# Seven block products in place of eight in the down projection of the second feed-forward

## The reference, cut to what matters

```
y = jnp.square(jax.nn.relu(h @ ffn_w1[i])) @ ffn_w2[i]
x = x + g2 * rmsnorm(y, norm_g[i, 3])
```

## Time and profile before

| | us |
|---|---|
| median of 3 runs | 2071.27 (2071.01 to 2071.88) |
| span of the profiled execution | 2068.0 |
| PE busy | 2035.2 (98%) |
| DVE busy | 1153.0 (56%) |
| ACT busy | 859.5 (42%) |
| POOL busy | 110.2 (5%) |
| chain that ended last: on PE | 94% |
| `ffn1`, from its first up tile to its last down tile | about 345 |

### The profile page before, as it was taken

One profiled execution on the slowest core, in us unless ns is written; L12 is line 12 of the kernel. 1 busy time (PEld: TensorE's weight loads), 2 busy tenths in 40 slices (PEclk: granted clock), 3 DMA queues, 4 the chain that ended last, 5 costly groups with the idle time before them and its releaser, 6 DMA issues.

```text
span 2068.0 us, 27825 instructions
## 1 busy us (share of the span) xinstructions
PE 2035.2 (98%) x10894; PEld 1699.1 (82%) x10894; DVE 1153.0 (56%) x1758; ACT 859.5 (42%) x1291; POOL 110.2 (5%) x100
## 2 busy tenths in 40 slices
PE   7999999999999999999999999999999999999998
PEld 5898888888887888988888888876777798888887
DVE  4667867566565345654233335436679746546455
ACT  3334472424246222356233246345455545324233
POOL 0000000000001025110000001000111000000000
PEclk9999999999999999999999999999999999999999
DMA  9572337576553423423332331511132132323321
GB/s 315 163 242 85 127 111 238 192 226 198 171 167 115 152 77 102 113 82 102 102 101 83 101 112 56 150 52 31 45 117 84 43 112 96 109 81 102 102 72 71
DMA packets 230377, 248.32 MB, mean 120 GB/s; under 512 B 10978, under 2 KB 223357, under 8 KB 229365
## 3 DMA queue, kind: packets, MB, share of 16 engines
q1 hardware_dynamic: 187968, 202.45, 30.8%
q10 hardware_dynamic: 42293, 44.27, 6.6%
HBM read 237.63 MB, written 8.42 MB: 119 GB/s over the span
## 4 chain that ended last, share of the span: by engine, by line
PE 94%; DVE 2%; ACT 1%; DMA 1%; issue 1%; DVEq 1%; SPq 0%; ACTq 0%; POOL 0%; POOLq 0%
PE bank L615 37%; PE bank L687 32%; PE bank L789 4%; PE bank L1254 4%; PE bank L718 2%; PE bank L859 2%; PE bank L1226 1%; PE bank L1003 1%; PE bank L1237 1%; PE bank L1201 1%; PE bank L1310 1%; PE bank L1295 1%; PE bank L1204 1%; PE bank L1124 1%; PE bank L754 1%; DMA ada_head<-in_ada_w 1%
## 5 line engine op out<-in xcount | busy, mean ns | idle before, releaser
L615 PE MATMUL bank<-h_hi,w_both_hi 128*128 128x512 f32 x528 | 206.6, 391 | 0.0
L615 PE MATMUL bank<-h_hi,w_both_lo 128*128 128x512 f32 x528 | 205.5, 389 | 0.0
L615 PE MATMUL bank<-h_lo,w_both_hi 128*128 128x512 f32 x528 | 205.5, 389 | 0.0
L1380 ACT ACTIVATE u_both_hi<-raw 128x2048 fp32r<-128x2048 f32 x62 | 117.1, 1906 | 174.3 <-PE bank L687 134.4
L1988 DVE TENSOR_TENSOR u_both_lo<-raw,u_both_hi 128x2048 fp32r<-128x2048 f32 x62 | 141.6, 2290 | 84.9 <-ACT u_both_hi L1380 84.9
L1988 DVE TENSOR_TENSOR w_both_lo<-raw,w_both_hi 128x2048 fp32r<-128x2048 f32 x62 | 142.0, 2290 | 74.6 <-ACT w_both_hi L1380 74.5
L615 PE MATMUL bank<-h_hi,u_both_hi 128*128 128x512 f32 x464 | 180.9, 390 | 0.0
L615 PE MATMUL bank<-h_lo,u_both_hi 128*128 128x512 f32 x464 | 180.6, 389 | 0.0
L615 PE MATMUL bank<-h_hi,u_both_lo 128*128 128x512 f32 x464 | 180.6, 389 | 0.0
L1380 ACT ACTIVATE w_both_hi<-raw 128x2048 fp32r<-128x2048 f32 x62 | 117.4, 1907 | 143.5 <-PE bank L687 91.8
L687 PE MATMUL bank<-u_both_hi,g_hi 128*128 128x512 f32 x408 | 160.1, 392 | 0.0
(11 more groups left out here) (455 smaller groups left out, 4495.9 us busy)
## 6 DMA issues: line engine op xcount, KB each, us to landing
raw<-in_ffn_w SPq DMA_DIRECT2D x64, 1024.0 KB, 5.2
ada_raw<-in_ada_w ACTq DMA_DIRECT2D x40, 1024.0 KB, 5.2
raw<-in_w_up SPq DMA_DIRECT2D x22, 1024.0 KB, 5.1
raw<-in_b_w_in SPq DMA_DIRECT2D x16, 1024.0 KB, 5.4
raw<-in_w_in SPq DMA_DIRECT2D x15, 1024.0 KB, 5.5
raw<-in_a_w_in SPq DMA_DIRECT2D x12, 1024.0 KB, 6.4
ada_head<-in_ada_w SPq DMA_DIRECT2D x8, 1024.0 KB, 12.3
raw<-in_b_w_out SPq DMA_DIRECT2D x8, 1024.0 KB, 6.3
```

Source lines behind the costliest of these rows:

```text
L615: mm = pe.matmul(o, x, y, start=(k == 0 and j == 0), stop=(k == kc - 1 and j == 2))
L1380: act.activation(slot(where, s)[0], raw[s][:], ACT.Copy).then_inc(sem("hi_done"), 1)
```

## The change

In groups 0, 1 and 2 of `ffn1` (`FAST = 3`) the down half is worked as one step of a Strassen-Winograd scheme. The hidden values of a group are a matrix A of 512 tokens x 1024, cut in quarters (`quarter(tok, k)`), the weights a matrix B of 1024 x 1024, cut in quarters B11, B12, B21, B22 of 512 x 512 (one 1 MB tile each). In place of eight products of quarters there are seven, m0 to m6, of quarters or sums of quarters. A product is 2 token blocks x 4 k-steps x 3 passes = 24 matmuls with 512 moving columns, so the down half has 168 matmuls in place of 192. The fourth group stays as it was.

Items of a group in PE's order, each with a split weight tile: u0, u1, u2, u3 (the up tiles, items 0 to 3), then m0 to m6 (items 4 to 10). Item by item the B side is B11, T1, T2, B22, T3, B21, T4, where the sums are made in place in the raw buffers by POOL with 128x2048 additions: T1 = B11 + B12, T2 = T1 + B22, T3 = B12 + B22, T4 = T2 + B21. POOL also makes `lo` of items 7 (B22) and 9 (B21), and one A-side difference S3 (128x1024). On the A side the hidden values are kept in full (`g32`: Relu and Square, no rounding); for each product ACT rounds a quarter or a sum into one of three `a_slot`s (128x1024) and DVE makes its `lo`; DVE makes the sums S1 (in two halves of 128x512), S2 and the next one (128x1024 each) in `s_sum`. Four raw buffers stand in place of two, and a ring of three split slots (W0, W1, U0) in place of four, because U1 is the room of raw buffers 2 and 3.

Products use banks 0 and 1 (even m) or 2 and 3 (odd m) and partly go on adding to what the bank holds. DVE adds the bank of each token block to `Y` after each product: 14 additions in a group in place of 8, and PE starts product m only when those of product m-2 are done. On PE, DVE, ACT and POOL the three groups are written out, without the loop. The rest of the change only merges semaphores.

```diff
-PHASES = [("a_in", 12, 2), ("a_out", 4, 2), ("ffn0", 32, 2), ("b_in", 16, 2), ("b_out", 8, 2), ("ffn1", 32, 2),
+PHASES = [("a_in", 12, 2), ("a_out", 4, 2), ("ffn0", 32, 2), ("b_in", 16, 2), ("b_out", 8, 2), ("ffn1", 10, 2),
...
+FAST = 3
+FAST_RING = [("W", 0), ("W", 1), ("U", 0)]
+FAST_NAMES = ["u0", "u1", "u2", "u3", "B11", "B12", "B22", "B21"]
+FAST_RAW = [[0, 1, 0, 1, 2, 3, 0, 1], [0, 3, 1, 2, 0, 3, 1, 2], [1, 3, 2, 0, 1, 3, 2, 0]]
+FAST_FROM = ["B11", "B11", "B11", "B22", "B12", "B21", "B11"]
+FAST_POOL = ["T1", "S3", "T2", "T3", "lo B22", "T4", "lo B21"]
...
+def fast_low(g, i):
+    if i in (7, 9):
+        return "f_pool", 7 * g + FAST_POOL.index("lo B22" if i == 7 else "lo B21") + 1
+    return "f_lo", sum(1 for n in range(2, 11 * g + i + 1) if n % 11 not in (7, 9))
...
+        f_raw = raw + [at("raw2", "U", [P, TILE], F32, 8192), at("raw3", "U", [P, TILE], F32, 24576)]
+        g32 = at("g_full", "G", [P, KB, S])
+        a_slot = [[at(f"a_{part}{i}", reg, [P, 4, HALF], F32R, off + 4096 * j) for j, part in enumerate(("hi", "lo"))]
+                  for i, (reg, off) in enumerate((("G", 16384), ("G", 24576), ("AD", 0)))]
+        s_sum = at("s_sum", "S2", [P, 4, HALF])
+        s3_sum = at("s3_sum", "C", [P, 4, HALF])
...
+        def fast_slot(n):
+            return slot(*FAST_RING[n % 3])
+        def quarter(tok, k):
+            return g32[:, 4 * k:4 * k + 4, tok * HALF:tok * HALF + HALF]
...
+            def fast_split(g, i):
+                which, n = fast_low(g, i)
+                sp.wait_ge(sem(which), n)
+            for g in range(FAST):
+                if g == 0:
+                    sp.wait_ge(sem("split_done"), t0 + 1)
+                else:
+                    fast_split(g - 1, 7)
+                    sp.wait_ge(sem("f_pool"), fast_pool(g - 1, "T3"))
+                    fast_in(g, "u0", cols(w1, g * 1024, 256))
+                    fast_split(g - 1, 8)
+                    fast_in(g, "u1", cols(w1, g * 1024 + 256, 256))
+                    fast_split(g - 1, 9)
+                    sp.wait_ge(sem("f_pool"), fast_pool(g - 1, "T4"))
+                fast_in(g, "u2", cols(w1, g * 1024 + 512, 256))
+                if g == 0:
+                    sp.wait_ge(sem("split_done"), t0 + 2)
+                else:
+                    fast_split(g - 1, 10)
+                fast_in(g, "u3", cols(w1, g * 1024 + 768, 256))
+                rows = cols(w2[:, g, :], 0, D)
+                if g == 0:
+                    sp.wait_ge(sem("block_done"), N0["ffn1"])
+                else:
+                    fast_split(g, 0)
+                fast_in(g, "B11", rows[:, 0:4, 0:512])
+                if g:
+                    fast_split(g, 1)
+                fast_in(g, "B12", rows[:, 0:4, 512:1024])
+                fast_split(g, 2)
+                fast_in(g, "B22", rows[:, 4:8, 512:1024])
+                fast_split(g, 3)
+                fast_in(g, "B21", rows[:, 4:8, 0:512])
...
+            def fast_up(g, j):
+                which, n = fast_low(g, j)
+                pe.wait_ge(sem(which), n)
+                wh, wl = (w.rearrange("p (k n) -> p k n", k=KB) for w in fast_slot(11 * g + j))
+                for b in range(2):
+                    m, bs = 2 * (j % 2) + b, slice(b * P, b * P + P)
+                    if j < 2:
+                        pe.wait_ge(sem("f_added"), 14 * g - (1 - b if j == 0 else 3 - b))
+                    else:
+                        pe.wait_ge(sem("f_g"), 8 * g + m + 1)
...
+            def fast_product(g, m):
+                which, n = fast_low(g, 4 + m)
+                pe.wait_ge(sem(which), n)
+                pe.wait_ge(sem("f_a_lo"), 8 * g + [1, 3, 4, 5, 6, 7, 8][m])
+                wh, wl = (w.rearrange("p (k n) -> p k n", k=4) for w in fast_slot(11 * g + 4 + m))
+                ah, al = a_slot[(7 * g + m) % 3]
+                for c in range(2):
+                    if m < 2:
+                        pe.wait_ge(sem("f_g"), 8 * g + 4 + 2 * m + c + 1)
+                    else:
+                        pe.wait_ge(sem("f_added"), 14 * g + 2 * (m - 2) + c + 1)
+                    cs = slice(c * P, c * P + P)
+                    for k in range(4):
+                        for i, (x, y) in enumerate([(ah, wh), (ah, wl), (al, wh)]):
+                            mm = pe.matmul(bank[2 * (m % 2) + c][:], x[:, k, cs], y[:, k], start=(k == i == 0 and m in (0, 1, 5)),
+                                           stop=(k == 3 and i == 2), skip_group_check=True)
+                    mm.then_inc(sem("f_product"), 1)
...
+            for g in range(FAST):
+                for j in range(0 if g else 2, 4):
+                    fast_up(g, j)
+                for m in range(7):
+                    fast_product(g, m)
...
+            def fast_free(n):
+                g, i = divmod(n - 3, 11)
+                if n == 2:
+                    act.wait_ge(sem("block_done"), 4 * q0)
+                elif n < 5:
+                    act.wait_ge(sem("block_done"), 4 * q0 + 2 * i + 2)
+                elif i < 4:
+                    act.wait_ge(sem("f_up"), fast_block(g, 2 * i + 1))
+                else:
+                    act.wait_ge(sem("f_product"), 14 * g + 2 * (i - 4) + 2)
...
+            for g in range(FAST):
+                fast_hi(g, 2)
+                fast_hidden(g, 0)
+                fast_hidden(g, 1)
+                fast_hi(g, 3)
+                fast_hidden(g, 2)
+                fast_hidden(g, 3)
+                fast_hi(g, 4)
+                act.drain()
+                fast_a(g, 0, quarter(0, 0))
+                fast_hidden(g, 4)
+                fast_hidden(g, 5)
+                fast_hi(g, 5)
+                act.wait_ge(sem("f_s"), 4 * g + 1)
+                fast_a(g, 1, s_sum, slice(0, 2))
+                fast_hidden(g, 6)
+                fast_hidden(g, 7)
+                act.wait_ge(sem("f_s"), 4 * g + 2)
+                fast_a(g, 1, s_sum, slice(2, 4))
+                fast_hi(g, 6)
+                act.wait_ge(sem("f_s"), 4 * g + 3)
+                fast_a(g, 2, s_sum)
+                fast_hi(g, 7)
+                act.wait_ge(sem("f_s"), 4 * g + 4)
+                fast_a(g, 3, s_sum)
+                fast_hi(g, 8)
+                act.wait_ge(sem("f_pool"), fast_pool(g, "S3"))
+                fast_a(g, 4, s3_sum)
+                fast_hi(g, 9)
+                fast_a(g, 5, quarter(0, 1))
+                fast_hi(g, 10)
+                fast_a(g, 6, quarter(1, 1))
+                for i in range(2):
+                    if g < FAST - 1:
+                        fast_hi(g + 1, i)
...
+            def fast_s1(g, ks):
+                dve.wait_ge(sem("f_g"), 8 * g + 4 + ks.stop)
+                dve.tensor_tensor(s_sum[:, ks], quarter(1, 0)[:, ks], quarter(1, 1)[:, ks], ALU.subtract).then_inc(sem("f_s"), 1)
...
+            def fast_add(g, m, c, row, part, op):
+                dve.wait_ge(sem("f_product"), 14 * g + 2 * m + c + 1)
+                o, b = Y[:, row + c, part * 512:part * 512 + 512], bank[2 * (m % 2) + c]
+                if g == 0 and m in (0, 1, 6):
+                    dve.tensor_copy(o, b[:]).then_inc(sem("f_added"), 1)
+                elif g == 0 and m == 2:
+                    dve.tensor_scalar(o, b[:], -1.0, None, ALU.mult).then_inc(sem("f_added"), 1)
+                else:
+                    dve.tensor_tensor(o, o, b[:], op).then_inc(sem("f_added"), 1)
...
+            for g in range(FAST):
+                for i in (2, 3, 4):
+                    fast_lo(g, i)
+                fast_a_lo(g, 0, 1, quarter(0, 0))
+                fast_lo(g, 5)
+                fast_s1(g, slice(0, 2))
+                fast_a_lo(g, 1, 2, s_sum, slice(0, 2))
+                fast_s1(g, slice(2, 4))
+                fast_a_lo(g, 1, 3, s_sum, slice(2, 4))
+                dve.drain()
+                dve.tensor_tensor(s_sum[:], s_sum[:], quarter(0, 0), ALU.subtract).then_inc(sem("f_s"), 1)
+                fast_lo(g, 6)
+                fast_a_lo(g, 2, 4, s_sum)
+                for c in range(2):
+                    fast_add(g, 0, c, 0, 0, ALU.add)
+                dve.tensor_tensor(s_sum[:], s_sum[:], quarter(0, 1), ALU.add).then_inc(sem("f_s"), 1)
+                for c in range(2):
+                    fast_add(g, 1, c, 2, 1, ALU.add)
+                fast_a_lo(g, 3, 5, s_sum)
+                fast_lo(g, 8)
+                fast_a_lo(g, 4, 6, s3_sum)
+                for c in range(2):
+                    fast_add(g, 2, c, 0, 1, ALU.subtract)
+                fast_a_lo(g, 5, 7, quarter(0, 1))
+                dve.drain()
+                for c in range(2):
+                    fast_add(g, 3, c, 0, 1, ALU.add)
+                fast_lo(g, 10)
+                fast_a_lo(g, 6, 8, quarter(1, 1))
+                for c in range(2):
+                    fast_add(g, 4, c, 2, 1, ALU.subtract)
+                if g < FAST - 1:
+                    fast_lo(g + 1, 0)
+                else:
+                    rest(u0, 0, "W")
+                for c in range(2):
```

(74 more changed lines are left out.)

106 lines of the change are left out of this document (89 added, 17 removed).

## The result

The changed kernel takes 2085.76 us (median of 4 runs, 2082.66 to 2086.99), the kernel before 2071.14 (4 runs): a ratio of 1.0072, 95% interval 1.0058 to 1.0085, so 0.7% slower. The forecast was 2085.0, 2075 to 2095.

What follows compares the result with a forecast made beforehand. The prediction took ffn1 as bound by PE's number of matmuls, 0.2267 us each. From 2068.0, -16.3 for matmuls and +30 for stalls gave 2081.7; with 3.3 from span to median, 2085.0 us, range 2075 to 2095.

Steps and rivals of the forecast that it cites:

- The rate and the matmuls: Three down halves of ffn1: 72 matmuls fewer at an unchanged 0.2267 us each, 16.3 us saved.
- What was costed at nothing: Groups 0 to 2: leaving the loop, added DVE and ACT work, split slots and loads, all covered by PE's matmuls.
- The exclusion: POOL and DVE instructions with two SBUF inputs hold each other off whole; +30 us in three groups, chance 0.74.
- two short cases: Profile before: DVE's 2.28 us lo stretched POOL's 1.28 to 3.39; POOL's instruction stretched DVE's 0.68 to 1.18.
- the stepping: One down half worked through instruction by instruction: stalls 1.8, 5.3 and 3.2 us, 10.3 a group, 31 in three.
- the releaser it named: The gaps before m1 and m3 were to end with DVE's lo of a_slot; no separate size.
- The third gap: Before m4: additions of m2 stand behind a lo held by POOL's lo of B21; 3.2 us a group.
- the first two gaps: Before m1 and m3: DVE's sums and lo wait for POOL's long instructions; 1.8 and 5.3 us a group.
- The sum: Whole kernel: -16.3 + 30 = +13.7 us, giving 2081.7 for the span and 2085.0 for the median.
- No exclusion for long instructions: Rival: POOL's long instructions don't hold DVE off, nothing is late, 16.3 us won in full, 2055; chance 0.13.
- In part: Rival: DVE is let in within a long POOL instruction; 2 to 5 us a group, 2061 to 2070; chance 0.06.
- Something more: Rival: also POOL's fp32r lo or in-place addition takes 5.0 us or more; +22, 2093 and above; chance 0.07.

Runs made afterwards that it cites:

- the first experiment: Changed kernel with POOL's six 128x2048 instructions of each group cut to 16 columns, all waits kept: 2056.13 us, ratio 0.9928 to the kernel before.
- the run with memsets: Changed kernel with POOL's six 128x2048 instructions of a group replaced by memsets of the same tiles: 2056.53 us, ratio 0.9936 to the kernel before.
- the last experiment: Changed kernel with DVE's two additions of m2 to Y moved ahead of the lo of product 4: 2082.40 us, ratio 1.0062 to the kernel before.
- with quarters: Changed kernel with each of POOL's 128x2048 instructions cut into four of 128x512: 2083.63 us, ratio 1.0064 to the kernel before.
- With halves: Changed kernel with each of POOL's 128x2048 instructions cut into two of 128x1024: 2072.85 us, ratio 1.0012 to the kernel before.

## Why the prediction was right

**The rate and the matmuls.** -16.3 us for 72 matmuls at 0.2267 us: the runs without exclusion show 38.08 us for 168, and `ffn1` from the end of its first pair to its last down tile takes 266.59 us in the first experiment (945.74 to 1212.33) against 282.90 before, 16.3 less.

**What was costed at nothing** (leaving the loop, 14 us more work for DVE and 9 for ACT in a group, three slots, the loads) is nothing: the same run has all of it and no gap.

**The exclusion.** The reading of two short cases carried over to 4.6 us instructions. The gaps before m1 and m3 stand in all three groups, where the stepping put them; the profile puts them down to `issue`, but m1 and m3 start 0.1 us behind the end of DVE's `lo` of `a_slot` (1065.82 and 1081.53 in the second group), the releaser it named. The third gap is there in the first two groups, released by an addition to `Y`, and all but gone in the last (0.1). The table counts groups from 0, so group 1 is the second.

| group 1 | stepped | measured |
|---|---|---|
| before m1 | 1.8 | 1.4 |
| before m3 | 5.3 | 4.7 |
| before m4 | 3.2 | 0.7 |
| m3 at a lower clock | 0 | 2.2 |
| group longer than 81.6 | 10.3 | 9.3 |
| three groups | 31, taken as 30 | 28.0 |

The rows of the second group add up to 9.0; the first matmuls behind a gap follow each other more slowly (0.31 us from the one of 1089.99 to the next in place of 0.2267), which is part of the other 0.3.

(28.0: from 946.49 to 1197.49 are 251.0 us, and 984 matmuls at 0.2267 are 223.0.) The rule of the Trainium skill, SBUF — State Buffer, section Summary: rules for kernel authors, that the one that issues second is blocked until the first has finished, agrees with the trace: DVE's third sum of 1071.59, 1.22 us long by itself, waited until POOL's 4.82 us were over. The same page, section Who interferes with whom, says that a DVE instruction with two SBUF inputs contends with a GpSimd instruction that reads SBUF and not with one that only writes; the run with memsets agrees (1.22 us beside 1.81).

**What was mis-sized.** POOL holds DVE for 4.4 us from the moment DVE lets it in, not 4.5 to 4.6, and ACT's 128x1024 copy takes 1.06 in place of 1.14; worked through the same steps these make up about the 1.0 us by which the first two gaps are shorter. The third gap was forecast at 3.2 and is 0.7: after 4.7 us without work PE ran m3 slower, and so it came to m4 later by itself. As m4 waits for a fixed chain on DVE, the slower matmuls were free. The three groups bear this out: m3 takes 1.6, 2.2 and 2.8 us more than its 5.44, the gap before m4 is 1.3, 0.7 and 0.1, and the sum is 2.9 each time. The prediction had no term for the clock; that it cost nothing here is luck.

**The sum.** The stage is 11.6 us longer where 13.7 were forecast (946.49 to 1241.01 is 294.52, before 282.90). The profiled execution is 12.9 longer as a whole, the medians 14.6. The close hit of the median, 2085.8 against 2085.0, is therefore partly luck: stalls forecast 2 us too long, and some 3 us that the sum didn't have. Of these, 1.3 lie outside the stage in the two profiled executions (12.9 against 11.6), nearly all behind it. The rest is in the other three executions, whose spans are 2083.7 to 2085.2 and whose mean granted clock is 0.991 to 0.993, against 0.994 in the profiled one and 0.997 before. That more of PE's work ran at the lower clock there is likely; no profile of them shows where. The experiments show one such place, though the kernel is the same there in all: in seven of the eight profiles the 10 us that begin 90 us after the start of the fourth group's down half have a granted clock of 0.83 or 0.84. Here they are in the last experiment, and below it in the changed kernel (the first value after the stretch's length is PE's busy time with the number of matmuls, the third from the end is the granted clock):

```profile
1327.55:1337.55 10.00, 10.00 (x51) 8.52 (x50) 3.26 (x5) 2.40 (x2) 2.03 (x2) 0.83 0.24 78
...
1331.01:1341.01 10.00, 10.00 (x58) 8.69 (x57) 3.25 (x5) 2.40 (x2) 2.03 (x2) 1.00 0.24 77
```

7 matmuls fewer in 10 us are 1.6 us. From the start of the fourth group's down half to the end the kernel before takes 838.8 us, the changed kernel 839.9, the eight experiments 841.5 to 843.6. So a part of each experiment's time is not the stage's, and a difference of some 2 us between two of them can come from there.

**The rivals.** No exclusion for long instructions: refuted by the durations. In part: in the three groups no DVE instruction with two SBUF inputs that came second ended before POOL's. Something more: POOL's in-place additions and its `lo` into fp32r take 4.62 and 4.63 us where nothing holds them (the run with DVE's operand in PSUM), the same as the row they were costed by.

## What to carry to other kernels

Before giving elementwise work to POOL, look whether DVE has two-input SBUF instructions in the same stretch. If so, each POOL instruction that reads SBUF is also a stall of DVE of up to its whole length, and of all that stands behind in DVE's list; compare that length with the shortest deadline on DVE, not its busy time with the span. The same sums on DVE itself, or on POOL only as far as they fit in the half with room on DVE, turned a change that loses 0.7% into one that wins 0.6%. Cutting POOL's instructions helps only until the pieces themselves wait too often.

## What was not expected of the hardware

PE's clock fell after a gap, within a stage that is otherwise at 2.4 GHz. Windows of the changed kernel: m1 and the start of m2; the rest of m2, the gap and the start of m3; the rest of m3 and the gap before m4; m4 to m6 (the value after the busy times is the granted clock). The last line is m3 right behind the gap by itself:

```profile
core 0: us, PE busy (x) PEld busy (x) DVE busy (x) ACT busy (x) POOL busy (x), PEclk, DMA share, GB/s
...
1066.00:1073.00 7.00, 7.00 (x31) 5.79 (x32) 7.00 (x6) 3.77 (x3) 2.88 (x1) 1.00 0.01 2
1073.00:1083.00 10.00, 5.45 (x22) 4.20 (x21) 10.00 (x5) 6.55 (x5) 8.70 (x3) 0.82 0.33 105
1083.00:1090.00 7.00, 6.47 (x23) 4.86 (x21) 7.00 (x4) 0.44 (x1) 5.16 (x1) 0.77 0.56 169
1090.00:1106.59 16.59, 16.59 (x73) 13.74 (x74) 13.65 (x13) 6.27 (x4) 0.00 (x0) 1.00 0.53 182
...
1081.60:1085.60 4.00, 3.97 (x9) 3.14 (x10) 4.00 (x2) 1.01 (x2) 3.86 (x1) 0.50 0.17 34
```

and the first matmuls behind the gap (start, us):

```profile
1076.70 0.39 PE L1271 MATMUL bank<-u_both_hi,a_lo 128*128 128x512 f32 x1
1081.63 0.76 PE L1271 MATMUL bank<-w_both_hi,a_hi 128*128 128x512 f32 x1 [4.55 <-issue]
...
1082.62 0.63 PE L1271 MATMUL bank<-w_both_hi,a_lo 128*128 128x512 f32 x1
1083.05 0.63 PE L1271 MATMUL bank<-w_both_hi,a_hi 128*128 128x512 f32 x1
```

0.43 us from start to start in place of 0.2267, and a granted clock of 0.50: the 1.2 GHz level, granted for a few microseconds behind the 4.7 us gap; behind the 1.4 us gap before m1 the clock stayed at 1.00. The slower matmuls cost 2.2 us in this group. Here a later wait hid them; where nothing waits behind, they come on top of the gap, 3.0 and 1.9 us in the first two groups with quarters.

The length of the gap alone doesn't tell whether the clock falls. With halves the gap before m4 is 2.8 us in each of the three groups: behind the first one the granted clock is 0.76 (992.74 to 1000.00) and the 72 matmuls of m4 to m6 take 18.20 us, behind the other two it is 1.00 and they take 16.6. What decides between these is open.
